# Order of ScalarE's copies and exponentials, place of the rope angles and of the dense bias rows in a one-layer attention and experts kernel

## Chip, cores and metric

The kernel runs on one core of a Trainium2 chip. The metric is the device time of one execution in microseconds (us), as a median of several. Lower is better.

## What is computed

One layer for 512 tokens of width 1024 in float32. RMSNorm, one combined projection, then two attentions with a causal mask by chunks of 64 tokens. Group A (8 heads of 64) selects for each query the 128 keys with the highest indexer score; group B (4 heads, two softmax maps each) subtracts the second map times a learned factor. Rotary embedding turns the first 16 dimensions of each head. Then output projection, residual, RMSNorm, and 4 of 32 experts per token with biases.

```
h = rms_norm(x); proj = h @ w_in            # iq, ik, iw, aq, ak, av, bq, bk, bv
cos, sin = rope_tables(positions)           # angle = position * inv_freq
A: score = sum_h relu(iq_h . ik) * iw_h;  p = softmax(q.k over the top keys);  y = p v
B: p1 - lam * p2, each a softmax;  y = rms_norm((p1 - lam p2) v)
x = x + [yA, yB] @ w_o
gates = softmax(top4(rms_norm(x) @ w_router + b_router))
expert e: gu = xb @ w_gu[e] + b_gu[e];  act = min(glu,7) * sigmoid(1.702 glu) * (clip(lin)+1)
out += gate * (act @ w_down[e] + b_down[e])
```

## The kernel before

**Numbers in two parts.** TensorE multiplies fp32r values. A float32 operand is therefore split: ScalarE copies it to fp32r (the upper part, `w_hi`, `split_hi`), VectorE subtracts that copy from the value (the lower part, `w_lo`, `split_lo`), and TensorE makes three products (L1708 to L1710, and L1946 for the experts).

**A written-out order.** `make_plan` builds one list of steps, `PLAN`. Each engine walks through this list in order and does its own part of each step, or nothing if it has none; semaphores connect the engines. So a step's place in `PLAN` sets its place in the queue of every engine that takes part in it.

**The start.** x and the first four pieces of `w_in` are loaded by SP, the positions by ScalarE's queue. The step `angles` is done by VectorE (L1450 to L1463: positions times frequencies, reduced to one turn, a chain of small operations, each waiting for the one before) and then ScalarE (L1005, L1006: two sines, with a table load ahead). `turn_h` transposes x on TensorE (L1720); ScalarE (L998) and VectorE (L1293) copy it out of PSUM as upper and lower part. `w_hi` is L1011, `w_lo` L568. The projections of items 0 and 1 are interleaved with the four pieces of the first weight chunk. `setup` (L1467 to L1489 on VectorE, an exponential at L1135 on ScalarE with a table load ahead) prepares the factor lambda, the tables of sines and cosines times gains and the router's weights. The first user of the tables is `rope` of item 0. Items are pairs of a chunk of projection columns and a tile of 128 tokens; item 3 is the first of chunk kvi.

**The attention.** It has 64 units, numbered n. In slot n, `attend(n)` puts the steps of several units one behind the other:

- `score` n: TensorE computes the scores (L1775 to L1782) in one of two PSUM banks; VectorE takes the row maximum (L1397); ScalarE takes the exponential with a row sum (L1089). The next use of the bank waits for the exponential.
- `combine` of the B product of unit n-1: VectorE (L1405 to L1409).
- from n = 24 on a weight piece, `w_hi` and `w_lo`; from n = 32 on a round of the top-k search (`topk`, L1385, L1386, VectorE). Before, these rounds stand between the parts of the projections.
- `turn_p` of the product of unit n-2: TensorE transposes the probabilities (L1720) in one of two banks, ScalarE copies them to SBUF (L1099), into the tile rel for the first 20 products and into sq for the other 28. A bank is shared with the transposes of heads, of y and of x1 (`turn_heads`, `turn_y`, `turn_x1`), two banks in turn.
- `values` of the product of unit n-3: TensorE multiplies them with the values (L1811), and waits for their copy.

```
plan.append(("score", n))
if product_of(n - 1) and product_of(n - 1)[0] == "B": plan.append(("combine", product_of(n - 1)))
if n >= 24: ... plan.append(("w_hi", pieces.pop(0))) ... lower()
if n >= 32: next_search(1)
if product_of(n - 2): plan.append(("turn_p", product_of(n - 2)))
if product_of(n - 3): plan.append(("values", product_of(n - 3)))
```

**The experts.** Each expert's weights come in 12 chunks of 1 MB, 8 for gate and up (`gate_up`), 4 for down (`down`). A chunk is loaded by SP into one of 8 buffers, split by ScalarE (L768) and VectorE (L773) into one of 4, and used by TensorE in 12 matmuls (L1946). Tokens are gathered by POOL (L928), transposed (`turn_x`, L1907); the activation is made by ScalarE (L1214) and VectorE (L1636, L1643, L1647). The down products of expert i-1 stand behind the gate and up products of expert i; expert 0 has none before it, so that TensorE goes from `gate_up(0)` and `turn_x(1)` to expert 1's bias (L1956), which waits for expert 0's activation.

**Dense bias rows.** The down biases of all experts, weighted by the gates, are a product of its own per tile of 128 tokens, made in four blocks: `dense_bias(t)` on TensorE (L1933, four matmuls of 512 columns into the two banks of the down products), `dense_rows(t)` on ScalarE (L1187, a copy into ysb), `add_dense(t)` on POOL (L945, an accumulating write into the output). `dense_bias(t)` waits for the rows before it, `dense_rows(t)` for the write of the rows before it, and `down(0)` for all four rows. `DENSE_AT` says behind which expert and chunk each block stands; ScalarE's places are written into `act_round`. VectorE hands out expert 3's slots (L1604, L1610) behind the split of chunk 9 of expert 0, and `turn_x(2)` waits for that.

## Time and profile before

| | us |
|---|---|
| median of 3 runs | 1535.85 |
| the runs | 1535.85, 1530.27, 1537.57 |
| the profiled execution | 1530.62 |
| its span in the profile | 1528.4 |
| TensorE busy | 1462.6 |
| VectorE busy | 1311.3 |
| ScalarE busy | 1104.2 |
| POOL busy | 238.6 |

The profile is of one execution. Its times count from the start of the span. PE is TensorE's matmuls, PEld its weight loads, DVE VectorE, ACT ScalarE, POOL GpSimd, SP the queue that issues most loads; L12 is line 12 of the kernel. An idle time is put down to the instruction that ended it.
### The profile page before, as it was taken

The page shows a single profiled execution, that of the slowest core. Times are in us where ns is not written, and L with a number is a line of the kernel's source. Part 1 is how long each engine was busy: PE and PEld are TensorE (multiplying, and loading weights), DVE is VectorE, ACT ScalarE, POOL GpSimd, SP SyncE. Part 2 cuts the span into 40 slices and gives each one's busy share as a digit, 9 for nine tenths or more (in the row PEclk, how much of TensorE's full clock was granted, in tenths as well). Part 3 has the DMA queues.
Part 4 walks back from the last instruction along what each step waited for, and adds up shares of the span by engine and source line. Part 5 has one row for each costly group of instructions (what it writes and reads, how often), then busy time and mean ns, then how long its engine had stood idle before and what let it go on. Part 6 is the DMA issues. An engine that isn't in the chain of part 4 may idle for free.

```text
span 1528.4 us, 18823 instructions
## 1 busy us (share of the span) xinstructions
PE 1462.6 (96%) x7148; PEld 1202.2 (79%) x7148; DVE 1311.3 (86%) x1320; ACT 1104.2 (72%) x1197; POOL 238.6 (16%) x120
## 2 busy tenths in 40 slices
PE   6999878998999999999999999999999999999996
PEld 5887667775778888888888888888888888888885
DVE  4799777548699999999999999999999999989995
ACT  5675555345677877787788877778777877887774
POOL 1221000011112111111211111121111122111101
PEclk9999969999999999999999999999999999999999
DMA  5422011148999999999999999999999999999991
GB/s 144 149 60 68 28 56 42 42 171 331 313 345 372 375 373 358 364 366 374 367 368 370 370 371 366 373 373 373 370 355 368 370 367 366 370 366 361 383 357 42
DMA packets 102307, 448.53 MB, mean 293 GB/s; under 512 B 18496, under 2 KB 23616, under 8 KB 69376
## 3 DMA queue, kind: packets, MB, share of 16 engines
q1 hardware_dynamic: 89808, 428.32, 72.7%
q0 software_dynamic: 9792, 18.90, 5.2%
q8 instruction: 59, 0.97, 0.2%
q10 hardware_dynamic: 2608, 0.01, 0.1%
q14 instruction: 40, 0.33, 0.1%
HBM read 440.89 MB, written 23.07 MB: 304 GB/s over the span
## 4 chain that ended last, share of the span: by engine, by line
PE 87%; DVE 6%; ACT 2%; DMA 2%; issue 1%; POOL 0%; SPq 0%; ACTq 0%; DVEq 0%; POOLq 0%
PE ps L1946 69%; PE ps L1708 2%; PE ps L1710 2%; PE ps L1709 2%; PE ps L1956 2%; PE ps L1720 2%; PE ps L1907 2%; PE ps L1915 2%; PE ps L1811 1%; DVE work L1386 1%; DVE nmax L1397 1%; DVE top L1385 1%; DMA posi<-in_positions_dram 1%; PE ps L1782 1%; DMA h_rows<-WR 0%
## 5 line engine op out<-in xcount | busy, mean ns | idle before, releaser
L773 DVE TENSOR_TENSOR whl<-wraw,whl 128x2048 fp32r<-128x2048 f32 x384 | 865.8, 2289 | 87.1 <-ACT whl L768 78.6
L768 ACT ACTIVATE whl<-wraw 128x2048 fp32r<-128x2048 f32 x384 | 732.6, 1918 | 207.2 <-PE ps L1946 207.2
L1946 PE MATMUL ps<-whl,xT 128*128 128x512 f32 x3120 | 732.3, 393 | 1.3 <-issue 1.3
L1946 PEld LDWEIGHTS ps<-whl,xT 128*128 128x128 f32 x3120 | 582.1, 188 | 122.7 <-issue 2.4
L1946 PE MATMUL ps<-whl,aT 128*128 128x512 f32 x1488 | 345.9, 392 | 0.0
L1946 PEld LDWEIGHTS ps<-whl,aT 128*128 128x128 f32 x1488 | 277.1, 188 | 56.1 <-DVE whl L773 0.3
L937 POOL DMA_INDIRECT out_dram<-ysb,idx x32 | 100.4, 3136 | 451.0 <-ACT ysb L1222 437.6
L928 POOL DMA_INDIRECT xg<-h_rows,idx x32 | 90.7, 2834 | 481.0 <-DVE idx L1604 464.7
L1708 PE MATMUL ps<-W,HT 128*128 128x512 f32 (+1 forms) x184 | 73.0, 397 | 7.5 <-DVE W L568 6.5
L1710 PE MATMUL ps<-W,HT 128*128 128x512 f32 (+1 forms) x184 | 69.4, 377 | 0.0
L1709 PE MATMUL ps<-W,HT 128*128 128x512 f32 (+1 forms) x184 | 69.3, 377 | 0.0
L1397 DVE TENSOR_REDUCE nmax<-ps 128x1 f32<-128x128 f32 (+3 forms) x64 | 31.2, 488 | 38.1 <-PE ps L1782 37.3
L1089 ACT ACTIVATE raw<-ps,nmax 128x384 f32<-128x384 f32 (+2 forms) x40 | 24.1, 601 | 50.8 <-DVE nmax L1397 50.7
L1214 ACT ACTIVATE acts<-ps 128x1024 f32<-128x1024 f32 x32 | 32.8, 1026 | 25.7 <-PE ps L1946 25.7
L1708 PEld LDWEIGHTS ps<-W,HT 128*128 128x128 f32 x184 | 35.7, 194 | 12.9 <-issue 6.9
L1616 DVE TENSOR_TENSOR xT<-ps,xT 128x512 fp32r<-128x512 f32 x64 | 41.0, 681 | 2.4 <-ACT xT L1195 2.4
L1222 ACT ACTIVATE ysb<-ps,gslot 128x1024 f32<-128x1024 f32 x32 | 35.1, 1096 | 10.2 <-PE ps L1946 10.2
L900 POOL TENSOR_TENSOR rstd<-ss,half 128x8 f32<-128x8 f32 (+1 forms) x16 | 26.1, 1629 | 104.0 <-DVE ss L1319 104.0
L1195 ACT ACTIVATE xT<-ps 128x512 fp32r<-128x512 f32 x64 | 34.7, 598 | 9.8 <-PE ps L1907 9.8
L1710 PEld LDWEIGHTS ps<-W,HT 128*128 128x128 f32 x184 | 35.4, 192 | 6.6
L1647 DVE SCALAR_TENSOR_TENSOR acts<-ps,acts 128x1024 f32<-128x1024 f32 x32 | 39.2, 1225 | 1.1
L1636 DVE TENSOR_SCALAR acts<-ps 128x1024 f32<-128x1024 f32 x32 | 39.0, 1218 | 0.9 <-PE ps L1946 0.9
(248 smaller groups left out, 1367.9 us busy)
## 6 DMA issues: line engine op xcount, KB each, us to landing
wraw<-in_w_gu_dram SPq DMA_DIRECT2D x256, 1024.0 KB, 8.0
wraw<-in_w_down_dram SPq DMA_DIRECT2D x128, 1024.0 KB, 7.4
WR<-in_w_in_dram SPq DMA_DIRECT2D x20, 512.0 KB, 3.7
WR<-in_w_o_dram SPq DMA_DIRECT2D x8, 512.0 KB, 3.7
xs<-in_x_dram SPq DMA_DIRECT2D x4, 512.0 KB, 7.6
WR<-in_x_dram SPq DMA_DIRECT2D x4, 512.0 KB, 3.4
out_dram<-WR SPq DMA_DIRECT2D x4, 512.0 KB, 2.6
h_rows<-WR SPq DMA_DIRECT2D x4, 512.0 KB, 2.8
```

The source lines that it names most:

```text
L768: act.activation(whl[:, n % HL, 0, :], wraw[n % RAW], ACT.Copy).then_inc(chunk_hi, 1)
L773: eng.tensor_tensor(whl[:, n % HL, 1, :], wraw[n % RAW], whl[:, n % HL, 0, :].bitcast(F32), ALU.subtract).then_inc(chunk_lo, 1)
L928: pool.indirect_dma_start(xg[j % 2], None, hd, bass.IndirectOffsetOnAxis(ap=idx[:, j:j + 1], axis=0), bounds_check=SEQ - 1, oob_is_err=Fal ...
L937: pool.indirect_dma_start(out[0], bass.IndirectOffsetOnAxis(ap=idx[:, e:e + 1], axis=0), ysb, None, bounds_check=SEQ - 1, oob_is_err=False ...
L1397: dve.tensor_reduce(nmax[:, t % 2, j:j + 1], ps[:, S_BANK + v % 2, 0:keys_of(t)], AX.X, ALU.max, negate=True).then_inc(max_ok, 1)
L1616: dve.tensor_tensor(xT[:, 1, 4 * b:4 * b + 4, :], ps[:, TP + b, :].rearrange("p (k n) -> p k n", k=4), xT[:, 0, 4 * b:4 * b + 4, :].bitcas ...
L1636: dve.tensor_scalar(acts[:, 1, :].rearrange("p (a n) -> p a n", a=2), ps[:, GU + 2:GU + 4, :], LIMIT + 1.0, 1.0 - LIMIT, ALU.min, ALU.max) ...
L1647: dve.scalar_tensor_tensor(out=acts[:, 2, :].rearrange("p (a n) -> p a n", a=2), in0=ps[:, GU:GU + 2, :], scalar=LIMIT, in1=acts[:, 1, :]. ...
L1708: pe.matmul(dst, a[0], b[0], start=k_first, stop=False)
L1709: pe.matmul(dst, a[0], b[1], start=False, stop=False)
L1710: return pe.matmul(dst, a[1], b[0], start=False, stop=k_last)
L1946: ins = pe.matmul(bank, a[x_][j], w[:, b, j, 512 * q:512 * q + 512], start=c == NG and j == 0 and n == 0, stop=last and j == nj - 1 and n ...
```

## The change

- The step `angles` moves from ahead of the first transposes to behind the projections of items 0 and 1, just ahead of `setup`.
- `turn_p` of n-2 moves ahead of the weight pieces and the search round. ScalarE's exponential gets a step `exp` of its own behind it; the step `score` no longer has a part on ScalarE. On TensorE and VectorE the order of the attention stays as it was.
- The second dense block moves from behind chunk 5 of expert 0 to behind `turn_x(1)`, the fourth from behind chunk 3 of expert 1 to behind chunk 5. The fourth copy of dense rows on ScalarE moves from behind the split of chunk 7 of expert 1 to behind that of chunk 9 (`NG + 1`) of expert 0.

```diff
@@ -122,7 +122,7 @@
     for m in range(4):
         pieces.remove(m)
         if m == 0:
-            plan += [("angles",), ("turn_h", 0, FIRST), ("turn_h", 1, FIRST)]
+            plan += [("turn_h", 0, FIRST), ("turn_h", 1, FIRST)]
         plan += [("w_hi", m), ("w_lo", m)]
         if m == 0:
             plan += [("turn_h", 2, FIRST), ("turn_h", 3, FIRST)]
@@ -132,7 +132,7 @@
         if m == 3:
             plan += [("turn_h", 2, REST), ("turn_h", 3, REST)]
         plan += [("proj", 1, m)]
-    plan += [("setup",)]
+    plan += [("angles",), ("setup",)]
     scores = [("iscore", t, h) for t in range(1, T) for h in range(HI)]
     search = [("topk", t, r) for t in range(1, T) for r in range(ROUNDS_TOPK)]
 
@@ -161,14 +161,16 @@
             plan.append(("score", n))
         if product_of(n - 1) and product_of(n - 1)[0] == "B":
             plan.append(("combine", product_of(n - 1)))
+        if product_of(n - 2):
+            plan.append(("turn_p", product_of(n - 2)))
+        if n < UNITS:
+            plan.append(("exp", n))
         if n >= 24:
             if pieces:
                 plan.append(("w_hi", pieces.pop(0)))
             lower()
         if n >= 32:
             next_search(1)
-        if product_of(n - 2):
-            plan.append(("turn_p", product_of(n - 2)))
         if product_of(n - 3):
             plan.append(("values", product_of(n - 3)))
         for st in LATE.get(n, []):
@@ -273,7 +275,7 @@
 RAW, HL = 8, 4
 LEAD = 2
 SIG_TOP = 1.0 / (1.0 + math.exp(-ALPHA * LIMIT))
-DENSE_AT = [(0, 3), (0, 5), (1, 1), (1, 3)]
+DENSE_AT = [(0, 3), (0, NG), (1, 1), (1, 5)]
 ROUNDS = SEQ // P
 
 
@@ -1063,8 +1065,8 @@
                         act.wait_ge(rel_used, v - 1)
                     act.activation(rel[:, v % 2, 0:w], ps[:, S_BANK + v % 2, 0:w], ACT.Relu) \
                        .then_inc(score_read, 1)
-                elif kind == "score":
-                    n, v = st[1], SCORE[st]
+                elif kind == "exp":
+                    n, v = st[1], SCORE[("score", st[1])]
                     t, j = unit(n)
                     w = keys_of(t)
                     act.wait_ge(max_ok, n + 1)
@@ -1254,10 +1256,12 @@
                         if c == 6:
                             if i + 1 < E:
                                 pick_gu(r, i + 1)
-                        if is0(r) and i == 1 and c in (2, 5, 7):
-                            dense_rows((2, 5, 7).index(c) + 1)
+                        if is0(r) and i == 1 and c in (2, 5):
+                            dense_rows((2, 5).index(c) + 1)
                     for c in range(NG, NCH - 1):
                         split_hi(act, r, i - 1, c)
+                        if is0(r) and i == 1 and c == NG + 1:
+                            dense_rows(3)
                     sigmoid(r, i)
                     if i + 1 < E:
                         turn_x_hi(r, i + 1)
@@ -2009,6 +2013,8 @@
                 gate_up_bias(r, 0)
                 gate_up(r, 0)
                 turn_x(r, 1)
+                if is0(r):
+                    dense_bias(DENSE_AT.index((0, NG)))
                 for i in range(1, E):
                     gate_up(r, i)
                     if i + 1 < E:
```

## Rows read from the trace of the kernel before

**Rows 1.** The page, part 4 (the chain that ended last), by engine.
```profile
PE 87%; DVE 6%; ACT 2%; DMA 2%; issue 1%; POOL 0%; SPq 0%; ACTq 0%; DVEq 0%; POOLq 0%
```

**Rows 2.** Windows: length, busy PE, PEld, DVE, ACT, POOL, granted clock, DMA share, GB/s.
```profile
118.00:196.00 78.00, 69.29 (x399) 57.03 (x400) 62.95 (x164) 43.92 (x103) 8.18 (x5) 0.98 0.16 48
196.00:221.00 25.00, 17.16 (x77) 13.49 (x75) 20.34 (x49) 16.43 (x48) 1.01 (x1) 0.66 0.20 64
360.00:1480.00 1120.00, 1115.67 (x5241) 919.36 (x5240) 1028.01 (x655) 885.81 (x745) 187.03 (x65) 1.00 0.96 365
```

**Rows 3.** Timeline of ScalarE: start, duration, line, operation, [idle before <-releaser].
```profile
13.19 0.23 ACT L1005 ACTIVATE sinr<-ang 128x32 f32<-128x32 f32 x1 [3.97 <-DVE cyc L1463]
...
13.44 1.55 ACT L998 ACTIVATE HT<-ps,gcol 128x256 fp32r<-128x256 f32 x4
...
33.64 1.28 ACT L1135 ACT_TABLE_LOAD   x1
```

**Rows 4.** Timeline of VectorE, the first 36 us.
```profile
9.40 0.17 DVE L1450 CAST posf<-posi 128x4 f32<-128x4 int32 x1 [9.40 <-DMA posi<-in_positions_dram]
...
35.24 0.16 DVE L1472 TENSOR_TENSOR lams<-lams 128x1 f32<-128x1 f32 x1 [0.62 <-ACT lams L1135]
```

**Rows 5.** Timeline of TensorE, the first 36 us.
```profile
7.12 3.68 PE L1720 MATMUL ps<-ident,xs 128*128 128x128 f32 x16 [7.12 <-POOL zero L889]
17.34 0.77 PE L1708 MATMUL ps<-W,HT 128*128 128x512 f32 x1 [6.54 <-DVE W L568]
...
22.97 0.39 PE L1709 MATMUL ps<-W,HT 128*128 128x512 f32 x1
```

**Rows 6.** Tile WR, first 5 us: its loads, and their time to landing.
```profile
L809 SPq DMA_DIRECT2D WR<-in_w_in_dram x4: 427/530/981, 1.7 to 3.8; - x4
...
DMA to landing us min/median/max: 6.5/7.8/9.0
```

**Rows 7.** Line 1089, the exponentials: what ended the idle time before them.
```profile
  DVE nmax L1397: 80.3, 54
```

**Rows 8.** TensorE's waits for line 1099, 60 to 345 us: total, times, longest.
```profile
PE ps L1720 <- ACT sq L1099: 5.5, 3, 2.5
PE ps L1811 <- ACT rel L1099: 5.2, 5, 2.0
PE ps L1720 <- ACT rel L1099: 5.0, 6, 1.3
PE ps L1811 <- ACT sq L1099: 3.5, 5, 1.6
```

**Rows 9.** Groups of ScalarE: the copies (busy us, mean ns, idle before).
```profile
L1099 ACT ACTIVATE sq<-ps 128x384 f32<-128x384 f32 (+2 forms) x28 | 14.4, 513 | 2.1 <-PE ps L1720 2.1
...
L1099 ACT ACTIVATE rel<-ps 128x128 f32<-128x128 f32 (+1 forms) x20 | 6.2, 311 | 0.0
```

**Rows 10.** Timeline of ScalarE, 148 to 158 us.
```profile
153.61 0.47 ACT L1089 ACTIVATE rel<-ps,nmax 128x256 f32<-128x256 f32 x1 [1.53 <-DVE nmax L1397]
```

**Rows 11.** Timeline of TensorE in four places.
```profile
154.50 1.14 PE L1720 MATMUL ps<-ident,stk 128*128 128x128 f32 x8 [1.27 <-ACT rel L1099]
...
249.98 0.63 PE L1720 MATMUL ps<-ident,WR 128*128 128x128 f32 x4 [2.45 <-ACT sq L1099]
...
393.86 1.16 PE L1956 MATMUL ps<-bgs,sel_gu 128*128 128x512 f32 x4 [3.12 <-DVE acts L1647]
...
423.69 1.09 PE L1907 MATMUL ps<-ident,xg 128*128 128x128 f32 x8 [1.21 <-DVE gslot L1610]
```

**Rows 12.** The chain that ended last, 380 to 436 us: start, duration, what.
```profile
382.98 1.13 PE ps L1933 x4
...
417.00 1.92 ACT whl L768
```

**Rows 13.** A window after that wait; columns as in rows 2.
```profile
395.00:398.00 3.00, 3.00 (x8) 2.43 (x8) 3.00 (x2) 1.41 (x1) 0.85 (x1) 0.50 0.82 184
```

**Rows 14.** Timeline of ScalarE: the last dense rows.
```profile
416.08 1.02 ACT L1187 ACTIVATE ysb<-ps 128x1024 f32<-128x1024 f32 x1 [4.07 <-DMA out_dram<-ysb]
```

## The prediction

> **What bounds the kernel now.** I read the chain that ended last first: 87% of it is TensorE, 6% VectorE, 2% ScalarE [rows 1]. Then the windows by stage. From 360 to 1480 us, the experts, TensorE is busy 1115.67 of 1120 us at the full clock [rows 2]: its matmuls alone set the pace, and an edit ahead of them shifts them as a whole. What the change can win lies before the steady part. In the attention, 118 to 196 us, TensorE is busy 69.29 of 78 us and VectorE 62.95, ScalarE only 43.92: neither of the first two is full, they wait for each other in turn. From 196 to 221 us TensorE has 17.16 of 25 us at a mean granted clock of 0.66, VectorE 20.34 [rows 2]. Then the waits: the exponentials of ScalarE wait 80.3 us in 54 times for VectorE's row maximum [rows 7], and TensorE waits 5.5 + 5.2 + 5.0 + 3.5 = 19.2 us in 19 times for ScalarE's copies of transposed probabilities [rows 8]. Last the two ends, the first 36 us and experts 0 and 1, as timelines and as the chain.
>
> **Rope angles.** Before, VectorE waits until 9.40 us for the positions [rows 4] and computes angles until the sine can start at 13.19 [rows 3]. ScalarE, which issues in order, has the sine ahead of the copies of the transposed x, so these start at 13.44 [rows 3], though TensorE's 16 transposes ran from 7.12 to 10.80 [rows 5]. The first projection starts at 17.34, after 6.54 us of idle [rows 5]. Without the angles ScalarE can start when the first four transposes are through, 7.12 + 3.68/4 = 8.0, say 8.1. That moves copies, splits and first projection by 13.44 - 8.1 = 5.3 us. The weight pieces allow it: issued from 1.7 to 3.8 and landed after 6.5 to 9.0 us, they are there between 8.2 and 12.8 [rows 6], and the first is wanted behind four copies at 8.1 + 1.55 = 9.7. The same vector work, 13.19 - 9.40 = 3.8 us, now stands between the second projection and the setup. ScalarE, and VectorE with it, came there at 33.64 [rows 3]; VectorE is now done with the angles at 33.64 - 5.3 + 3.8 = 32.1. On ScalarE the sine's table load hides under these 3.8 us, but the exponential's load of 1.28 us [rows 3] now comes after the sines (13.44 - 13.19, some 0.3) and no longer under the setup's first steps. From its start to VectorE's use of the exponential it was 35.24 - 33.64 = 1.6 us [rows 3, 4]; so that use comes at 32.1 + 0.3 + 1.6 = 34.0. Of the 5.3 us, 1.2 reach the rope and the next splits of weights; TensorE, which could have kept 5.3, meets these splits at the fourth item, the first of chunk kvi, and waits there. To this comes the clock: the matmul at 17.34 took 0.77 us, the one at 22.97 0.39 [rows 5]; I read the 5.6 us between as TensorE's lower level, 1.2 GHz. If that stretch is shorter when transposes and projection lie 1.3 us apart and not 6.5, half of what it loses is won: between 0 and 2.8 us. I take 0.6, near the lower end, since the rows show a restart and none with so short a gap. **Start: 1.8 us, ends 0 and 4.0.**
> The Trainium skill (ScalarE: Activation LUTs, section What ACT_TABLE_LOAD costs) budgets about 2.66 us for a switch of table set, load and drain. By that, an estimate, the second switch would take some 1.4 us more and the fixed part of the start would lose 0.2 us instead of winning 1.2; the trace has a load of 1.28 us and the exponential's result used 1.6 us after it began, so I keep that.
>
> **Copies ahead of exponentials.** Only ScalarE's order changes: TensorE and VectorE skip the new step, and the 48 copies and 64 exponentials stay. In a slot n the copy of product n-2 stood behind the exponential n, which waits for VectorE's maximum, and from slot 24 on behind a weight copy too. Now it waits only for TensorE's transposes. No DMA is issued by the moved step, and no queue of SP or POOL is passed. What is won is less than the wait. At 154.50 TensorE waits 1.27 us for a bank [rows 11] that a copy frees after an exponential which itself had idled 1.53 us [rows 10]. The copy will run in that idle time; but TensorE's next transposes, of heads, are read by ScalarE behind the same exponential, so TensorE wins little more than the copy's 0.31 us [rows 9] and one handover, 0.3 to 0.7. That is about a third of such a wait. The waits behind copies into rel, up to 203 us, are 5.2 + 5.0 = 10.2 us [rows 8]: 3.5. Those behind copies into sq, later, are 5.5 + 3.5 = 9.0 us [rows 8]. But VectorE is near full until 221 us [rows 2], TensorE is the limit after it, and the largest, like 2.45 us at 249.98 [rows 11], stand before transposes of y, whose two copies to SBUF follow the same two ScalarE instructions in either order: 0.5. **Attention: 4.0 us.** Ends: all 19.2 us [rows 8] on one side, and on the other a loss, rival B.
>
> **Dense bias rows.** A block of four matmuls costs 1.13 us [rows 12]. The second block moves out of expert 0's products, where TensorE has no gap, into the 3.12 us in which TensorE waits for the activation at 393.86 [rows 11]: 1.13 us won, and the gap shrinks to about 2 us. Were that cover gone, it would cost what it costs now. The fourth moves within expert 1 and its ScalarE copy behind two more splits. Before, that copy waited 4.07 us for the accumulating write of the rows before it [rows 14]; the splits behind it, from 417.00 [rows 12], were late, so was VectorE, and TensorE waited 1.21 us for it at 423.69 [rows 11]. Now splits go first, that write lands under them, and this wait is gone. Next late is nothing: the down products, which need these banks read, start about 3 us after the copy; POOL's fourth dense write moves by about 1 us, and behind it are only the gather for expert 3, wanted 30 us later, and the first expert scatter. The blocks' writes to HBM stay four. After the gap TensorE ran at half clock, 3 us of it in the window from 395 [rows 13], which costs about half of some 3.4 us, 1.7. With 2 us of idle in place of 3.1 it may or may not fall: I take 0.9. **Experts 0 and 1: 2.3 + 0.9 = 3.2 us, ends 1.1 and 4.1.**
>
> **Sum.** 1.8 + 4.0 + 3.2 = 9.0 us. The profiled execution took 1530.62 us (span 1528.4 and 2.2 around it), so its like would take 1521.6. It was near the fastest of the three runs; their median is 1535.85, and I put the forecast against that: 1526.9, say 1527.
>
> **Rivals.**
> A, VectorE takes the attention's gain: its maxima, top-k and splits are the bound, and each copy that comes early only lengthens TensorE's next wait. For it: VectorE's 62.95 of 78 and 20.34 of 25 us [rows 2]. Against it: the other 15 and 5 us are idle. Left are 1.2 + 2.3 = 3.5 us: 1532.3.
> B, slower: the exponential is held back. ScalarE is in order, so exponential n now also waits for TensorE's transposes of n-2 and the copy, and the next score bank, the combination and VectorE hang on it. Its place are slots in which VectorE is free and the maximum comes before the copy has ended. The copies are 14.4 + 6.2 = 20.6 us [rows 9]. If half of that lands on the path, 10.3 - 3.5 = 6.8 us are lost: 1542.7. It decides from 3.5/20.6 = 17% on. Against it: exponentials waited 80.3 us for the maximum [rows 7], four times what all copies take, and the copy can use that time.
> C, the clock answers to the smaller gaps. The mean of 0.66 from 196 to 221 us [rows 2] is 25 x 0.34/0.5 = 17 us at 1.2 GHz; if they go and a third of the 8.5 us of work they cost was on the path, 2.8 us are won, with the other half of the drop after 393.86 0.8 more, and with the start warm early 2.2 more: 1521. For it speak rows 13, at half clock after 3.12 us of idle; against it, that gaps of 1 to 2 us remain everywhere.
> The Trainium skill (TensorE: Matmul & The Clock Gate, section What's actually happening) says so too: the throttled state is the default and activity releases it.
> D, the angle move does nothing, as TensorE's new wait of some 3 us before the fourth item throttles it: 1.8 us less, 1528.7.
>
> **How the numbers follow.** A difference under 0.5%, 7.7 us, can't be told from none here. The forecast has a chance of 0.44; A 0.24; B 0.05; C 0.17; D 0.10. The forecast's 9.0 us lies just over the bound, so of its 0.44 I put 0.34 to faster and 0.10 to same; all of C, 0.03 of D and 0.02 of A make faster 0.56, the rest but B same, 0.39, and B slower, 0.05. The range reaches from C with some of the upper ends (1519) to beyond A (1534), and leaves B out.
>
> **What would show it.** In the profile after: first projection near 12 us and VectorE's setup near 32; TensorE's waits on line 1099's copies well under 19.2 us, exponentials idle less; no 1.21 us wait before expert 2's transposes, no 4.07 us before the last dense copy, and a gap near 2 us before expert 1. I am wrong if the steady part starts less than 5 us earlier, if the waits on copies fall but those on VectorE rise by as much (A), or if waits on the exponential appear (B).

## The result, and the profile after it

The changed kernel took 1520.92 us (median of 5 runs, 1518.60 to 1521.68) against 1531.78 us (median of 5, 1530.14 to 1537.57) of the kernel before. The ratio is 0.9915, its 95% interval 0.9896 to 0.9934: between 10 and 16 us, some 13 us, faster (the two medians differ by 10.9). The forecast had 9.0 us and a range that holds the measured time; the direction was right, the size was not. Its profiled execution took 1518.60 us (span 1516.4), 12.0 us less than the profiled one before.

Three marks are used from here on. **First mark**: VectorE's first use of the lambda exponential, the end of the start. **Second mark**: ScalarE's last copy of turned y, near the end of the attention. **Third mark**: TensorE's product with expert 2's bias, after which nothing differs: from there to the end of the span it takes 1092.6 to 1092.9 us in all fourteen profiles. Times of one execution each:

| execution | first mark | first to second | second to third | third mark |
|---|---|---|---|---|
| before | 35.24 | 298.09 | 102.35 | 435.68 |
| after | 31.85 | 292.80 | 99.05 | 423.70 |
| before less after | 3.39 | 5.29 | 3.30 | 11.98 |
| forecast | 1.8 | 4.0 | 3.2 | 9.0 |

The chain of the changed kernel by engine, the page's part 4, answers to [rows 1]:

```profile
PE 84%; DVE 9%; DMA 2%; ACT 2%; issue 2%; POOL 1%; SPq 0%; ACTq 0%; POOLq 0%; DVEq 0%
```

VectorE holds 9% of it in place of 6%: parts of the attention in which TensorE waited for ScalarE's copies hang on VectorE now. TensorE's waits say the same: between the first two marks those for ScalarE fell from 19.9 us to 11.4, those for VectorE rose from 7.0 to 15.7.

**Start.** Timelines of TensorE, ScalarE and VectorE, against [rows 3 to 5]:

```profile
12.34 0.47 PE L1712 MATMUL ps<-W,HT 128*128 128x512 f32 x1 [1.52 <-DVE W L570]
12.64 0.40 PE L1713 MATMUL ps<-W,HT 128*128 128x512 f32 x1
...
34.88 0.50 PE L1712 MATMUL ps<-W,HT 128*128 128x200 f32 x1 [2.88 <-DVE W L570]
```
```profile
8.30 1.69 ACT L1000 ACTIVATE HT<-ps,gcol 128x256 fp32r<-128x256 f32 x4 [0.31 <-PE ps L1724]
...
30.24 1.28 ACT L1137 ACT_TABLE_LOAD   x1
31.54 0.20 ACT L1137 ACTIVATE lams<-lams 128x2 f32<-128x2 f32 x1
```
```profile
31.85 0.16 DVE L1476 TENSOR_TENSOR lams<-lams 128x1 f32<-128x1 f32 x1 [1.17 <-ACT lams L1137]
```

The copies start at 8.30 in place of 13.44, the first projection at 12.34 in place of 17.34: the 5 us forecast. But its products take 0.47 and 0.40 us at once, where before they took 0.77 at first and came to 0.39 only at 22.97: TensorE is at 2.4 GHz when it begins. The new wait of 2.88 us before the last narrow projection is there too. On ScalarE the exponential's table load of 1.28 us stands behind the sines, and VectorE uses its result 1.6 us after the load began, as the forecast had from before. (The Trainium skill, ScalarE: Activation LUTs, section What ACT_TABLE_LOAD costs, budgets 2.66 us for that switch, load and drain. The load's part agrees with the 1.28 us here; a drain doesn't show, as the exponential starts at 31.54, 0.02 us after the load's end, so the measurement decides.)

**Attention.** The waits of ScalarE and TensorE (total, times, longest), against [rows 7, 8]:

```profile
ACT sq L1101 <- PE ps L1724: 28.7, 18, 2.9
...
ACT raw L1091 <- DVE nmax L1401: 19.1, 19, 3.3
ACT rel L1091 <- DVE nmax L1401: 17.1, 19, 3.1
...
ACT rel L1101 <- PE ps L1724: 11.9, 12, 2.8
...
PE ps L1724 <- ACT sq L1101: 4.3, 2, 2.5
...
PE ps L1724 <- ACT rel L1101: 2.9, 2, 2.1
PE ps L1724 <- ACT W L1060: 2.9, 4, 1.4
...
PE ps L1724 <- DVE raw L1413: 2.5, 4, 0.8
```

The exponentials waited 80.3 us for the maximum and now 19.1 + 17.1 = 36.2; the copies wait 28.7 + 11.9 = 40.6 us for the transposes, in time that was idle anyway. TensorE waited 19.2 us for copies and now 4.3 + 2.9 here and 1.0 in two shorter rows, 8.2 in all. Longer are waits for VectorE's scaled probabilities (2.5, before 0.4) and for ScalarE's copies of queries (2.9, before 0.7). The windows that answer to [rows 2], with the columns given there:

```profile
114.00:192.00 78.00, 70.50 (x414) 58.13 (x412) 65.56 (x171) 46.14 (x108) 8.19 (x5) 0.98 0.16 48
192.00:216.00 24.00, 16.79 (x68) 13.28 (x68) 19.79 (x48) 16.11 (x47) 1.01 (x1) 0.64 0.19 67
```

The second has a mean granted clock of 0.64, where it was 0.66: the long stretch at 1.2 GHz is still there.

**Experts 0 and 1.** Timelines of TensorE and ScalarE, against [rows 11, 14]; then the chain (start, duration, what):

```profile
384.04 1.18 PE L1960 MATMUL ps<-bgs,sel_gu 128*128 128x512 f32 x4 [2.00 <-DVE acts L1651]
...
410.77 1.04 PE L1911 MATMUL ps<-ident,xg 128*128 128x128 f32 x8
...
420.83 0.50 PE L1950 MATMUL ps<-whl,aT 128*128 128x512 f32 x1 [0.82 <-DVE whl L775]
```
```profile
408.69 1.03 ACT L1189 ACTIVATE ysb<-ps 128x1024 f32<-128x1024 f32 x1 [2.65 <-DMA out_dram<-ysb]
```
```profile
395.53 1.02 ACT ysb L1189
...
396.84 11.77 DMA out_dram<-ysb
...
409.62 1.92 ACT whl L770
...
411.56 2.29 DVE whl L775
...
418.57 2.21 DVE whl L775
```

The gap before expert 1 is 2.00 us in place of 3.12. The wait of 1.21 us before expert 2's transposes (410.77) is gone. In its place TensorE waits 0.82 us later, for VectorE's split of expert 0's last down chunk: behind it, in the chain, stands the accumulating write of the third rows, 11.77 us long, for which ScalarE waits 2.65. In the profile before, the same write was over 7.8 us after its issue.

### The profile page after: what moved, and what is told of

Read it like the earlier page. It is cut to its first block, busy times and chain, and to the rows that moved or that the text cites. A ratio compares the mean times of both kernels' runs of the same rounds, so it can differ in the third digit from the quotient of the medians.

```text
span 1516.4 us, 18820 instructions
## 1 busy us (share of the span) xinstructions
PE 1457.5 (96%) x7145; PEld 1199.4 (79%) x7148; DVE 1311.7 (87%) x1320; ACT 1106.8 (73%) x1197; POOL 236.5 (16%) x120
## 4 chain that ended last, share of the span: by engine, by line
PE 84%; DVE 9%; DMA 2%; ACT 2%; issue 2%; POOL 1%; SPq 0%; ACTq 0%; POOLq 0%; DVEq 0%
PE ps L1950 68%; PE ps L1960 2%; PE ps L1712 2%; PE ps L1919 2%; PE ps L1714 2%; PE ps L1713 2%; PE ps L1911 2%; PE ps L1724 2%; DVE work L1390 1%; DVE top L1389 1%; DVE nmax L1401 1%; PE ps L1815 1%; DVE W L570 1%; DMA out_dram<-ysb 1%; DMA h_rows<-WR 1%
## 5 line engine op out<-in xcount | busy, mean ns | idle before, releaser
L1224 ACT ACTIVATE ysb<-ps,gslot 128x1024 f32<-128x1024 f32 x32 | 35.1, 1098 | 10.2 <-PE ps L1950 10.2
L1633 DVE TENSOR_TENSOR aT<-ps,aT 128x512 fp32r<-128x512 f32 x62 | 39.7, 682 | 0.0
```

Of the source, the lines that this page charges most:

```text
L1633: dve.tensor_tensor(a_of(e)[:, 1, 4 * b:4 * b + 4, :], ps[:, TP + b, :].rearrange("p (k n) -> p k n", k=4), a_of(e)[:, 0, 4 * b:4 * b + 4, ...
```

## Experiments

Each is an edit of the kernel before (e1 to e6) or of the changed kernel (e7 to e10). Their marks are put together behind e6.

### e1: only the angles

```diff
-            plan += [("angles",), ("turn_h", 0, FIRST), ("turn_h", 1, FIRST)]
+            plan += [("turn_h", 0, FIRST), ("turn_h", 1, FIRST)]
...
-    plan += [("setup",)]
+    plan += [("angles",), ("setup",)]
```

> The kernel before with the angle step alone moved behind the second projection. Three marks are read: VectorE's first use of the lambda exponential (before 35.24, after the whole change 31.85), ScalarE's copy of the turned y of the last tile's half (333.33 and 324.65), and TensorE's bias product of expert 2 (435.68 and 423.70). My theory (the miss of the start is its clock term: TensorE comes to the first projection after 1.5 us of idle and not 6.5 us and is at full clock there): first projection near 12.3 with products of 0.39 us from the first on, first mark 31.9 (3.4 us won, of them 2.2 by the clock), second near 330, third near 432.3, so about 3.4 us in all. Rival (the clock at the start has to do with something else of the change): products of 0.63 us at the first projection, first mark near 34.0, 1.2 us won. Second rival: the 3.4 us of the start are lost again in the attention, whose waits have other reasons: first mark 31.9, second within 1 us of 333.3.

Median 1534.07 us of 10 runs against 1534.61 of 16; ratio 0.9985 [0.9970, 1.0000]. TensorE's timeline at the first projection, and two windows (columns of [rows 2]):

```profile
12.32 0.47 PE L1708 MATMUL ps<-W,HT 128*128 128x512 f32 x1 [1.92 <-DVE W L568]
12.62 0.40 PE L1709 MATMUL ps<-W,HT 128*128 128x512 f32 x1
```
```profile
13.40:16.60 3.20, 3.20 (x9) 2.52 (x8) 3.20 (x4) 3.20 (x5) 0.00 (x0) 0.50 0.81 228
119.20:122.40 3.20, 3.20 (x9) 2.53 (x9) 3.06 (x10) 1.12 (x2) 0.00 (x0) 0.50 0.57 166
```

The first projection starts at 12.32, at full clock, and 1 us later the clock falls to 0.50 for 3.4 us. A second half-clock stretch, of 6.8 us from 37.2, follows the new wait of 2.88 us; by 76 us the lead of 1.8 us has shrunk to 1.3. The first mark comes at 33.42, which is 1.8 us ahead of before: just the forecast's number, and neither of the two that I had written down. At 119 us, behind a wait of 1.09 us that TensorE has in both kernels, the clock falls again, which it did not do before. TensorE in the kernel before, then here:

```profile
119.96 0.66 PE L1720 MATMUL ps<-ident,stk 128*128 128x128 f32 x4 [1.09 <-ACT rel L1099]
```
```profile
118.62 0.72 PE L1720 MATMUL ps<-ident,stk 128*128 128x128 f32 x4 [1.09 <-ACT rel L1099]
```

At this point e1 is 1.34 us ahead; the next transpose of probabilities starts at 124.81 before and at 125.09 here, 0.28 us behind. So this fall costs 1.6 us, the second mark comes at 333.92, and in this execution nothing of the start's gain is left. It is the second slowest of the ten: by the ratio e1 is some 2 us faster, by the medians 0.5, which is not clear of none. The second rival is right in its outcome here. The third mark comes at 441.83, 6.2 us behind before, in a stretch of experts that the edit does not touch. ScalarE and TensorE there:

```profile
419.58 1.03 ACT L1187 ACTIVATE ysb<-ps 128x1024 f32<-128x1024 f32 x1 [6.94 <-DMA out_dram<-ysb]
```
```profile
427.19 1.11 PE L1907 MATMUL ps<-ident,xg 128*128 128x128 f32 x4 [4.08 <-DVE gslot L1610]
```

The same copy that had waited 4.07 us [rows 14] waits 6.94 us for the write, and TensorE 4.08 us where it had waited 1.21 [rows 11].

### e2: only the copies ahead of the exponentials

```diff
+        if product_of(n - 2):
+            plan.append(("turn_p", product_of(n - 2)))
+        if n < UNITS:
+            plan.append(("exp", n))
         if n >= 24:
...
-        if product_of(n - 2):
-            plan.append(("turn_p", product_of(n - 2)))
...
```

> The kernel before with the copies of probabilities ahead of the exponentials and nothing else. The start must stand as before (first mark 35.24). My theory (the parts add up; the attention term was mis-sized, 5.3 us and not 4.0): second mark 5.3 us ahead of before, near 328.0, third near 430.4. Rival (part of the attention's gain needs the shifted start): second mark near 329.3, 4.0 us won. By the clock, the half-clock time between 41 and 343 us should shrink by some 3 us from 34.

Median 1528.06 us of 7 runs; ratio 0.9961 [0.9944, 0.9978], 6.0 us. From first to second mark 292.83 us, against 292.80 in the whole change: the swap's 5.3 us need nothing of the other parts. VectorE's instructions against before: 0.97 us ahead at 36 us (the start's clock, no edit), 0.97 still at 123, 5.35 at 203, 7.44 at 250 and 6.23 at 302 us. So in this execution the copies into `rel` gave 4.4 us, where the forecast had 3.5, those into `sq` 0.9, where it had 0.5. The division is not firm: 1.7 of the 4.4 us come between 188 and 196 us, where the clock fell before (190.1 us) and did not fall here, and in after and e11, where it fell near 165 us, only 2.8 us were won up to the same instructions. My remark on the clock was wrong: the half-clock time of this stage is 34.1 us, as before.

### e3: the copy ahead of the weight copy, but behind the exponential

```diff
+        if product_of(n - 2):
+            plan.append(("turn_p", product_of(n - 2)))
         if n >= 24:
...
-        if product_of(n - 2):
-            plan.append(("turn_p", product_of(n - 2)))
```

> The kernel before with the copy behind the exponential still, but ahead of the weight copy that stands behind the exponential from slot 24 on. It splits the attention term: what comes from passing the exponential (all slots) and what from passing the weight copy (about 1.07 us each, slots 24 on). My theory: the exponential, which waits for the maximum, holds the copy up: up to slot 24 nothing changes, and of some 5.3 us at the second mark at most 1.5 are won (second mark 331.8 or later). Rival: the weight copy was what held it up: 3 us or more at the second mark, near 330 or earlier.

1533.43 us, one run. From first to second mark 296.94 us, 1.1 less than before. Up to 190 us nothing moved beyond the 0.4 us of the start. By this one execution the exponential was what held the copies up, for 4 of the 5.3 us.

### e4: TensorE kept busy ahead of the first projection

```diff
+                    if u == 0 and part == 0:
+                        keep_warm(14)
                     if u < 2:
```

> The kernel before with 14 products of 512 columns into a bank that nothing uses yet, on TensorE between the first sixteen transposes and the first projection, where it idles 6.5 us; the angles stay where they were. My theory of the start: this alone wins the clock term, so the products of the first projection take 0.39 us and not 0.63, TensorE ends its first two projections 2.6 us earlier, the first mark comes at about 32.9 (2.3 us won) with ScalarE's first copies still at 13.4. Rival: the lower clock at 17.34 does not come from the idle time ahead of it; products of 0.63 us, first mark at 35.2 or later.

1535.00 us, one run. TensorE's timeline:

```profile
10.28 3.18 PE L1715 MATMUL ps<-ones,identb 128*128 128x512 bf16 x14
17.32 0.77 PE L1708 MATMUL ps<-W,HT 128*128 128x512 f32 x1 [3.85 <-DVE W L568]
17.89 0.63 PE L1709 MATMUL ps<-W,HT 128*128 128x512 f32 x1
```

The 14 products took 0.23 us each, at full clock; 3.85 us of idle were left behind them, and the first projection again ran at 0.63 us a product, for 2.9 us in place of 5.5. First mark 33.95, 1.3 us ahead, lost again by 124 us as in e1, behind the same fall of the clock at 119 us. The test did not fill the gap, so it decides little between its two theories.

### e5: only the fourth dense block and its rows

```diff
-DENSE_AT = [(0, 3), (0, 5), (1, 1), (1, 3)]
+DENSE_AT = [(0, 3), (0, 5), (1, 1), (1, 5)]
...
-                        if is0(r) and i == 1 and c in (2, 5, 7):
-                            dense_rows((2, 5, 7).index(c) + 1)
+                        if is0(r) and i == 1 and c in (2, 5):
+                            dense_rows((2, 5).index(c) + 1)
                     for c in range(NG, NCH - 1):
                         split_hi(act, r, i - 1, c)
+                        if is0(r) and i == 1 and c == NG + 1:
+                            dense_rows(3)
```

> The kernel before with only the fourth dense block and its rows further back (block at chunk 5 of expert 1, rows after the second down split). The runs so far show that the wait for the write of the third rows is not 4.1 us each time: the last dense copy waited 4.07, 4.5, 6.9, 6.9 and 7.0 us in five executions with the old order, TensorE then 1.2, 1.6, 4.1, 4.0 and 4.2 us, and from the turned y (second mark) to expert 2's bias product (third mark) it took 102.35, 103.3, 107.9, 106.6 and 106.2 us; the whole change took 99.05. My theory: the largest part of what the forecast missed sits here, in the executions that were not profiled: this edit alone makes the stretch about 102 us whatever the write takes, so the median comes 3 to 5 us below the kernel before and the spread from fastest to slowest shrinks from 8 us to 4. Rival (the dense move is worth what its profiled 1.21 us said): median 1 to 1.5 us below before, spread as before.

Median 1528.46 us of 12 runs (1527.27 to 1530.44) against 1534.40 of 23 (1529.38 to 1538.08); ratio 0.9965 [0.9954, 0.9977], 5.4 us with 3.5 to 7.1, and a spread of 3.2 in place of 8.7 us. The stretch of experts takes 100.51 us. ScalarE's last dense copy and TensorE up to expert 2's transposes have no idle time left:

```profile
416.53 1.01 ACT L1187 ACTIVATE ysb<-ps 128x1024 f32<-128x1024 f32 x1
```
```profile
415.79 5.72 PE L1948 MATMUL ps<-whl,xT 128*128 128x512 f32 x24
421.34 1.04 PE L1909 MATMUL ps<-ident,xg 128*128 128x128 f32 x8
```

This is the measurement that gives the size. The rival, worth its profiled 1.2 us, falls.

### e6: only the second dense block

```diff
-DENSE_AT = [(0, 3), (0, 5), (1, 1), (1, 3)]
+DENSE_AT = [(0, 3), (0, NG), (1, 1), (1, 3)]
...
                 turn_x(r, 1)
+                if is0(r):
+                    dense_bias(DENSE_AT.index((0, NG)))
```

> The kernel before with only the second dense block moved into TensorE's wait for expert 0's activation. My theory: 1.13 us of products come off and the wait shrinks from 3.1 to 2.0 us; the whole change showed no half-clock time behind that wait, worth 1.7 us more: the stretch from the second to the third mark 2.9 us shorter, 99.5 where the write of the third rows lands early and about 104 where it lands late. Rival: the clock still drops behind a wait of 2 us; then 1.1 us shorter.

Median 1533.47 us of 10 runs; ratio 1.0000 [0.9988, 1.0012]: nothing. TensorE and ScalarE:

```profile
391.79 1.16 PE L1956 MATMUL ps<-bgs,sel_gu 128*128 128x512 f32 x4 [2.00 <-DVE acts L1647]
...
424.19 1.97 PE L1907 MATMUL ps<-ident,xg 128*128 128x128 f32 x8 [5.37 <-DVE gslot L1610]
```
```profile
416.58 1.03 ACT L1187 ACTIVATE ysb<-ps 128x1024 f32<-128x1024 f32 x1 [8.24 <-DMA out_dram<-ysb]
```

Up to expert 1's bias product the move works: 59.17 us from the second mark, against 60.2 to 61.0 in the six kernels with the old place, and the gap is 2.00 us. The clock doesn't fall behind that gap, so that at 398 us TensorE has won 2.8 us since 382. Then the write takes 12.0 us from its issue, and TensorE waits 5.37 us. Counted from the second mark, the write is issued at 72.0 us, where the kernels with the old place have 74.6 to 75.4; the copy that waits for it starts at 84.0, where they have 82.8 to 85.7. So in this execution an issue 3 us earlier brought no earlier landing. With the old order of splits, all that is won ahead of that write can be lost in the wait for it.

The marks of the executions with the old order of splits and rows, and of e5:

| execution | first | first to second | issue of the third rows' write to the last dense copy | TensorE's wait | second to third | us |
|---|---|---|---|---|---|---|
| before | 35.24 | 298.09 | 7.8 | 1.21 | 102.35 | 1530.62 |
| e2 | 34.27 | 292.83 | 8.3 | 1.65 | 103.29 | 1525.29 |
| e12 (before again) | 35.46 | 298.21 | 9.6 | 2.97 | 105.54 | 1534.11 |
| e3 | 35.00 | 296.94 | 10.6 | 4.0 | 106.65 | 1533.43 |
| e1 | 33.42 | 300.50 | 10.7 | 4.08 | 107.91 | 1536.56 |
| e4 | 33.95 | 300.06 | 10.8 | 4.2 | 106.16 | 1535.00 |
| e6 | 34.80 | 297.83 | 12.0 | 5.37 | 105.32 | 1532.70 |
| e5 | 34.75 | 297.86 | 9.1, not waited for | none | 100.51 | 1527.84 |

### e7: the angles where VectorE idles

```diff
-            plan += [("x_sum",), ("turn_h", 0, REST), ("turn_h", 1, REST)]
+            plan += [("x_sum",), ("angles",), ("turn_h", 0, REST), ("turn_h", 1, REST)]
...
-    plan += [("angles",), ("setup",)]
+    plan += [("setup",)]
```

> The changed kernel with the angle step moved again: to where VectorE idles 4.6 us in the start (17.5 to 22.1), between the sums of squares and the second half of the transposed x. In the changed kernel its 3.75 us of vector work and a second table load stand on the path to the rope. My theory (that step of the forecast was right, the angles cost 3.8 us on VectorE's path there): first mark 3.7 to 4.1 us ahead of the changed kernel's 31.85, near 28, no longer wait of ScalarE for the sine; second mark near 320.8; all in all 3.5 us below the changed kernel. Rival: TensorE's weight pieces or VectorE's later splits are the next bound and the attention takes it back, as it took the angle move's 1.8 us in the kernel with the old order of copies: second mark 323.5 or later, time the same as the changed kernel within 1 us.

Median 1515.36 us of 5 runs (1512.95 to 1519.15); ratio to before 0.9875 [0.9856, 0.9895]; 5.6 us under the changed kernel. The profile is of the slowest of them. VectorE, then TensorE at the first projection:

```profile
17.38 0.16 DVE L1454 CAST posf<-posi 128x4 f32<-128x4 int32 x1
...
25.00 1.66 DVE L1297 SCALAR_TENSOR_TENSOR HT<-ps,gcol,HT 128x256 fp32r<-128x256 f32 x4 [3.84 <-ACT HT L1000]
...
30.53 0.16 DVE L1476 TENSOR_TENSOR lams<-lams 128x1 f32<-128x1 f32 x1 [0.63 <-ACT lams L1137]
```
```profile
12.31 0.77 PE L1712 MATMUL ps<-W,HT 128*128 128x512 f32 x1 [1.52 <-DVE W L570]
12.88 0.63 PE L1713 MATMUL ps<-W,HT 128*128 128x512 f32 x1
...
18.00 0.62 PE L1713 MATMUL ps<-W,HT 128*128 128x512 f32 x1
18.42 0.43 PE L1714 MATMUL ps<-W,HT 128*128 128x512 f32 x1
```

The angles lie in idle time, 17.38 to 21.2, and 3.84 us of it are still left behind them. But here the products of the first projection take 0.63 us for six microseconds, although TensorE's wait before them is 1.52 us as in the changed kernel. So the first mark is 30.53 and not 28. The second mark comes at 324.74, where the rival had put it (323.5 or later); the median, 5.6 us lower and not the same, is against the rival, and is more than the 3.5 us expected.

### e8: the last dense copy one split later

```diff
-                        if is0(r) and i == 1 and c == NG + 1:
+                        if is0(r) and i == 1 and c == NG + 2:
                             dense_rows(3)
```

> The changed kernel with the last dense copy one split later still (after the third down split). In the changed kernel it waits 2.65 us for the write of the third rows, VectorE then 2.98 us and TensorE 0.82 us before expert 0's last down chunk. My theory: the third down split then runs under the write, the 0.82 us go, the stretch from the second to the third mark is 98.2 instead of 99.05, the end 0.8 us earlier. Rival: the down products of expert 0 wait for this copy in its place: stretch as before or longer, with TensorE waiting on the last dense copy.

Median 1518.89 us of 4 runs; ratio 0.9903 [0.9881, 0.9925]. TensorE goes from expert 2's transposes through all down products of expert 0 without a wait:

```profile
412.32 1.04 PE L1911 MATMUL ps<-ident,xg 128*128 128x128 f32 x8
413.12 11.18 PE L1950 MATMUL ps<-whl,aT 128*128 128x512 f32 x48
```

The stretch takes 97.89 us, 1.2 less than 99.05. The medians say 2 us, within their spread.

### e9 and e10: both later edits, and TensorE busy in its last 1.5 us of idle

> Both later edits on the changed kernel: angles in VectorE's idle 4.6 us, last dense copy behind the third down split. With the angles there the changed kernel ran at 1515.36 us (median) against 1520.92, with the later rows at 1518.89. My theory (the two sit at opposite ends of the stage and add up, as the parts of the change did): 1513 to 1514, stretch from second to third mark 97.9. First mark between 28.1 and 30.6, by the clock of the first projection, which came out full in one and partly at half in three of four executions that had the angles moved. Rival (what the angles win is lost when the clock draws badly, and 1515.36 was luck): 1516 to 1518, second mark at 324 or later.

Median 1514.38 us of 4 runs (1513.10 to 1516.13); ratio to before 0.9870 [0.9850, 0.9891]: 20 us under before, the best version found. First mark 28.96, second 321.55, stretch of experts 98.28. The sum is a little less than the parts, within their spread.

```diff
+                    if u == 0 and part == 0:
+                        keep_warm(6)
```

> As the kernel with both later edits, and six products of 512 columns on TensorE in its 1.5 us of idle between the first transposes and the first projection. Theory A: that short wait is what lets the clock stay low in some executions; the products of the first projection take 0.39 us from the first on in every look, first mark 28.1, median 1.5 us below the kernel without them and a narrower spread. Theory B: the clock comes up on its own after the transposes at a time that differs between executions, whatever TensorE does in 1.5 us; then no difference in the median beyond 1 us, and with the clock still low the six products take 2.6 us instead of 1.4 and push the first projection back by up to 1 us.

Median 1515.58 us of 4 runs (1514.03 to 1516.02), no faster than e9. TensorE:

```profile
10.61 2.71 PE L1719 MATMUL ps<-ones,identb 128*128 128x512 bf16 x6
12.82 0.73 PE L1712 MATMUL ps<-W,HT 128*128 128x512 f32 x1
13.39 0.40 PE L1713 MATMUL ps<-W,HT 128*128 128x512 f32 x1
```

The six products took 2.71 us, at half clock, and pushed the first projection back by 0.5 us. The clock then came up at 13.1. One profile cannot say whether they brought it up; the median says that they don't pay.

### e11 and e12: both kernels once more

> The changed kernel once more, for a second profile and for times beside the others on the same chip. If the start's clock is drawn anew in each execution, the first mark lies anywhere from 31.8 to 33.5; the stretch from first to second mark stays 292.8 within 0.3 (attention, the same in three executions of this order of copies), the one from second to third mark 99 to 99.6 although the write of the third rows takes 12 us. Median 1520 to 1521.5. Were my account wrong, the two stretches would vary by more than 1 us.

The changed kernel: 1521.22 us (median of 6, 1518.31 to 1522.64), ratio 0.9912 [0.9896, 0.9929], the first result again. First mark 33.43, first to second 294.54, second to third 98.71. The second number misses my bounds by 1.4 us, the third by 0.3. By my own sign, a stretch that varies by more than 1 us, my account was too exact: between these marks the granted clock was at 0.50 for 41.0 us, where it was for 34.1 in each of the three equal profiles (after, e2, e8); e7 and e10, with 37.5, took 294.2 and 294.4 us.

> The kernel before once more, for a second profile. My account (the profile on which the forecast rested was an execution with an early write of the third rows): with three of four late draws in the old order, the last dense copy waits about 7 us, TensorE about 4 us before expert 2's transposes, and from the second to the third mark it takes 106 to 108 us, where it was 102.35; the execution then takes 1533 to 1537 us. If it is 102 to 103.5 again, the early write is the usual case and the dense term was not the one that was mis-sized. First to second mark 297.9 within 0.5 in either case.

The kernel before: 1534.11 us. ScalarE's last dense copy and TensorE behind it:

```profile
418.11 1.03 ACT L1187 ACTIVATE ysb<-ps 128x1024 f32<-128x1024 f32 x1 [5.83 <-DMA out_dram<-ysb]
```
```profile
425.72 1.78 PE L1907 MATMUL ps<-ident,xg 128*128 128x128 f32 x8 [2.97 <-DVE gslot L1610]
```

First to second mark 298.21, second to third 105.54: later than in the profile on which the forecast rested (102.35), but short of the 106 to 108 expected, as is the wait of 2.97 us. One execution of the same kernel shows that the stretch varies by 3.2 us with no edit at all.

## Why the prediction was right and wrong

**What failed: the term for experts 0 and 1, 3.2 us.** The step is "this wait is gone", priced at the 1.21 us of [rows 11]. The mechanism was right: splits go first, the write lands under them, wholly in e5 and e8 and all but 2.65 us in after. The size was that of one execution, near the fastest of the runs then known. Over the six profiled executions of the old order with the second block in its old place (before, e1 to e4, e12) this stretch takes 105.3 us in the mean, with waits of 1.2 to 4.2 us (mean 3.0) and, behind four of them, a fall of the clock; in three with the changed order (after, e7, e11) 99.1. The whole term measures 6.2 us. The removed wait, priced at 1.21, is worth 5.4 (3.5 to 7.1) by the runs of e5, which has this edit alone. The two profiles that I had compared at first hid this: their difference there, 3.30 us, looks like the forecast's 3.2. It was also a mistake of method to subtract terms of a profile of 1530.62 from a median of 1535.85 without asking which wait makes up the 5 us between them. The five runs of the result put the kernel before at 1531.78, so that the 1527 forecast lies only 4.8 us below it, where the measured median lies 10.9 below.

**The second block**, 1.13 us and a gap of 2 us: both as forecast (TensorE gains 1.2 us there in after, e6, e7, e8 and e11), but worth nothing alone (e6), where the write landed no earlier. With the fourth block's move it seems to pay: the stretch is 99.1 us in the mean of three, against 100.51 in e5; no run has these two edits and no other. The clock term of 0.9 was too low as well: of seven executions with the 2.0 us gap the clock fell behind it in one (e11), of seven with 3.1 us in all, and where it did not fall TensorE gained 1.6 us against before (after, 9.8 us ahead at 394, 11.4 at 398). "Next late is nothing" was wrong by 0.82 us (after, e7); e8 takes that back.

**Attention, 4.0 us: mis-sized, somewhat under 5.** "That is about a third of such a wait" is the step. In e2, of the 10.2 us behind copies into `rel` 7 went and 4.4 were won, more than a third; in after and e11 only 2.8 were, so that this step is within what the clock moves. Of the 9.0 behind `sq` 4 went and 0.9 were won. The reason given, that the next transposes of heads hang on the same exponential, fits TensorE's wait for copies of queries, 2.9 us and before 0.7. In means of four profiles each the stage took 298.0 us (before, e5, e6, e12) and 293.2 (after, e2, e8, e11), 4.8 us less; in e2 alone 5.2, and with e7, e9 and e10, seven profiles of the new order, 4.6.

**Start, 1.8 us: right in the mean, by luck in the parts.** The first mark stood at 34.9 us in the mean of six executions with the old start (before, e2, e3, e5, e6, e12), at 33.0 of four with the new one (after, e1, e8, e11): 1.9 us. The clock term is no number but a draw: with a low clock for some time the new start won 1.5 us against that mean (e1, e8, e11), with a full one 3.1 (after); with the same 1.5 to 1.9 us of idle ahead, the first projection ran wholly at full clock (after), fell to half for 3.4 us (e1), or began at half until 15.2 to 18.5 us (e7, e8, e9, e11). The bounds of 0 and 2.8 were the honest statement. (The Trainium skill, TensorE: Matmul & The Clock Gate, section What's actually happening, says that the number of slow products at the start of one and the same kernel varies from run to run; these profiles agree.) Nor does the start's gain reach the end surely: with the old order of copies the profiled executions of e1 and e4 had lost it by 124 us.

Together: 1.9 + 4.8 + 6.2 = 12.9 us against the measured 13.0. The runs of the parts give the same: 0.9985 x 0.9961 x 0.9965 x 1.0000 = 0.9911, the whole 0.9915 and 0.9912. Each of these ratios is known to 0.001 or 0.002, so neither sum can show whether a part is worth 1 or 2 us more beside the others than alone.

**The rivals.** A, VectorE takes the gain: in part; of the 9.0 us by which TensorE's waits for ScalarE fell in e2, 6.1 came back as waits for VectorE, but some 5 us came through (3.6 us less idle time and 1.7 less busy time of TensorE between the first two marks, at the same 34.1 us of half clock). B, slower: no; the copies wait 40.6 us in time that was idle. C gave the right time, 1521, mostly for a wrong reason: the 17 us at low clock near 200 us are there with the change too (13.7 + 3.4 us), and the full clock at the start, its 2.2 us, held through the first projection in one execution of four (after, e1, e8, e11). Its 0.8 behind the gap were had in six of seven. D: the wait of 2.88 us and a half-clock stretch behind it are there (3.4 us in after, 6.8 in e1, e8 and e11), but most of the first mark's gain was kept: at 76 us 3.2 of 3.4 us in after, 1.3 of 1.8 in e1. Of the list of signs, two did not come true: VectorE began the setup at 29.8 and not 32, by the clock, and the last dense copy still waits 2.65 us.

**What stays open**: why the accumulating write of the third rows takes 7.8 us in one execution and 12.0 in another, and what its landing waits for, since with an issue 2 to 3 us earlier (e6, after, e7, e11) it took longer, 10.9 to 12.0 us, and came no sooner, and why in e1 and e4, and in no other kernel, the clock fell behind the wait of 1.09 us at 119 us. None of this was tried.

## What to carry to other kernels

A wait on a DMA's landing has no price but a distribution: when the runs before spread over 8 us and the profile is of the fastest, look for such waits, price their removal at the late landing, and expect a narrower spread as well as a lower median. A gain ahead of such a wait can be worth nothing until the wait itself is gone (e6), so changes that each measure zero or little alone can belong together. In an in-order engine, put what waits for work already done ahead of what waits for a slower engine; and when a step has to be moved off a path, look for the idle time into which it fits (VectorE's 4.6 us at 17.5) before putting it at the end.

## What the runs showed of the hardware

- A software-queue accumulating write of 512 KB took between 7.8 and 12.0 us from its issue to the copy that waited for it, for the same kernel 7.8 (before) and 9.6 (e12), beside weight loads (DMA share 0.90 from 343 to 436 us, before). In the one execution of e6, where it was issued 3 us earlier, it landed no earlier.
- TensorE's clock after the same history is not the same: after 3.67 to 3.68 us of transposes and 1.52 us of idle its products began at 0.47 us once (after) and at 0.76 to 0.77 us four times (e7, e8, e9, e11). Fourteen products of 0.23 us each and then 3.85 us of idle (e4) were followed by 3.4 us at half clock.
- Falls of the clock moved from one wait to another between executions (the first one of the attention came anywhere from 119 to 200 us), and the one at 119 us cost 1.6 us, in e1 and in e4; differences of 1 to 2 us between two profiles in such a stage mean little.
